# Order of the weight sums on GpSimd and of ScalarE's steps in a hybrid decoder block

## What is computed

```python
h = rmsnorm(x, norm_g)
proj = jnp.einsum('bsd,de->bse', h, w_in)
sb_q, sb_k, sb_v, sb_z, hg_q, hg_f, hg_i, hg_z, gate_logits = jnp.split(proj, split_points, axis=-1)
# stick-breaking attention, per head
z = jnp.einsum('bhqd,bhkd->bhqk', qb, kf) * scale
log_not = jnp.where(causal, jax.nn.log_sigmoid(-z), 0.0)
survive = lax.cumsum(log_not, axis=3, reverse=True) - log_not
w = jnp.exp(jnp.where(causal, jax.nn.log_sigmoid(z) + survive, -jnp.inf))
u_sb = jnp.einsum('bse,ed->bsd', sb_o * jax.nn.silu(sb_z), w_sb_proj)
# HGRN2, per head: a decayed linear attention with state, then rmsnorm
u_hg = jnp.einsum('bse,ed->bsd', hg_o * jax.nn.silu(hg_z), w_hg_proj)
y = gate_sb * u_sb + gate_hg * u_hg
x = x + jnp.einsum('bsd,de->bse', y, w_out)
out = rmsnorm(x, final_norm_g)
```

## Time and profile before

| | us |
|---|---|
| median of 3 runs | 1340.43 |
| lowest and highest | 1339.3, 1341.13 |
| the profiled execution | 1341.63 |
| its span, first to last instruction | 1339.9 |
| TensorE busy | 1320.7 |
| VectorE busy | 918.5 |
| GpSimd busy | 747.0 |
| ScalarE busy | 581.2 |

### The profile page before, as it was taken

One profiled execution on the slowest core, in us unless ns is written; L12 is line 12 of the kernel. 1 busy time (PEld: TensorE's weight loads), 2 busy tenths in 40 slices (PEclk: granted clock), 3 DMA queues, 4 the chain that ended last, 5 costly groups with the idle time before them and its releaser, 6 DMA issues.

```text
span 1339.9 us, 23157 instructions
## 1 busy us (share of the span) xinstructions
PE 1320.7 (99%) x8369; PEld 1101.5 (82%) x8369; DVE 918.5 (69%) x1078; ACT 581.2 (43%) x950; POOL 747.0 (56%) x511
## 2 busy tenths in 40 slices
PE   8999999999999999999999999999999999989998
PEld 7888788888888878888888887888887888878887
DVE  5848877876877887787687788778634446855323
ACT  7553355255345335525534533552444433443222
POOL 5655664554665566455466556645588722787300
PEclk9999999999999999999999999999999999999999
DMA  5121111311112111121111211113544479454602
GB/s 189 32 80 63 33 64 32 94 63 31 63 47 78 63 31 63 31 93 64 31 63 47 78 63 31 63 31 110 183 180 142 156 262 328 142 180 133 228 28 99
DMA packets 132651, 126.98 MB, mean 95 GB/s; under 512 B 4304, under 2 KB 110848, under 8 KB 132608
## 3 DMA queue, kind: packets, MB, share of 16 engines
q1 hardware_dynamic: 124432, 105.13, 24.6%
q10 hardware_dynamic: 8176, 21.26, 4.4%
HBM read 92.82 MB, written 33.55 MB: 94 GB/s over the span
## 4 chain that ended last, share of the span: by engine, by line
PE 79%; POOL 6%; ACT 5%; DVE 4%; issue 3%; DMA 1%; ACTq 0%; SPq 0%; DVEq 0%; POOLq 0%
PE banks L2042 44%; PE banks L2389 6%; PE banks L2337 5%; PE banks L2125 5%; PE banks L2375 5%; PE banks L2103 4%; PE banks L2115 2%; POOL b_lo L787 2%; POOL b_sum L787 2%; ACT b_hi L918 1%; PE banks L2184 1%; PE banks L2089 1%; PE banks L2165 1%; PE banks L2186 1%; PE banks L2179 1%
## 5 line engine op out<-in xcount | busy, mean ns | idle before, releaser
L2042 PE MATMUL banks<-a_hi,b_hi 128*128 128x512 f32 x1064 | 432.0, 406 | 1.7 <-POOL b_lo L787 1.7
L2042 PE MATMUL banks<-a_hi,b_lo 128*128 128x512 f32 x1064 | 416.6, 392 | 0.0
L2042 PE MATMUL banks<-a_lo,b_hi 128*128 128x512 f32 x1064 | 415.3, 390 | 0.0
L787 POOL TENSOR_TENSOR b_lo<-w_raw,b_hi 128x512 fp32r<-128x512 f32 x106 | 159.2, 1513 | 229.9 <-ACT b_hi L918 229.9
L787 POOL TENSOR_TENSOR b_lo<-b_sum,b_hi 128x512 fp32r<-128x512 f32 x114 | 165.7, 1453 | 145.5 <-ACT b_hi L918 145.4
L2042 PEld LDWEIGHTS banks<-a_hi,b_lo 128*128 128x128 f32 x1064 | 199.7, 188 | 44.0
L2042 PEld LDWEIGHTS banks<-a_hi,b_hi 128*128 128x128 f32 x1064 | 200.0, 188 | 41.3 <-POOL b_lo L787 2.9
L2042 PEld LDWEIGHTS banks<-a_lo,b_hi 128*128 128x128 f32 x1064 | 200.4, 188 | 35.8
L918 ACT ACTIVATE b_hi<-b_sum 128x512 fp32r<-128x512 f32 x114 | 71.9, 630 | 145.9 <-POOL b_sum L787 145.6
L787 POOL TENSOR_TENSOR b_sum<-w_raw 128x512 f32<-128x512 f32 x68 | 100.6, 1480 | 0.0
L1101 ACT ACTIVATE wT<-banks 128x512 f32<-128x512 f32 (+2 forms) x96 | 47.1, 491 | 104.5 <-PE banks L2115 88.7
(11 more groups left out here) (256 smaller groups left out, 2620.8 us busy)
## 6 DMA issues: line engine op xcount, KB each, us to landing
w_raw<-in_w_in SPq DMA_DIRECT2D x72, 512.0 KB, 4.9
gate_d<-gate_out SPq DMA_DIRECT2D x16, 512.0 KB, 3.5
x_tok<-in_x SPq DMA_DIRECT2D x8, 512.0 KB, 6.5
z_d<-z_out SPq DMA_DIRECT2D x8, 512.0 KB, 2.7
hz_d<-z_out SPq DMA_DIRECT2D x8, 512.0 KB, 2.7
osb_d<-o_sb SPq DMA_DIRECT2D x8, 512.0 KB, 5.6
ohg_d<-hq SPq DMA_DIRECT2D x8, 512.0 KB, 2.7
w_other<-in_w_in SPq DMA_DIRECT2D x8, 512.0 KB, 5.7
```

The lines of the kernel that those rows point to most:

```text
L787: return nc.gpsimd.tensor_tensor(dst, a, b, op)
L2042: last = mm(bank, w[:, s, k, :], t[s][:, k, :], start=opens and k == 0 and z == 0, stop=k == QUAD - 1 and z == 2, skip_group_check=not opens)
```

## The change

GpSimd now makes T5, T6 and T7 in this order right after the low part of P1, and then the low parts of P6, P7 and P5 in the order of the products. `SPLIT_ORDER` and the numbers of the sums follow this, also in the hg pairs. ScalarE splits P7 at point 10 instead of 7, P5 at 11, P2 at 12 and P3 at 13, one point later each; P6 stays at 9 and P1 at 6. In the hg branch `branch_high` of P2 and P3 stand ahead of the splits of the first hg pair, its split of P7 comes a panel later, and at point 1 the copy of P1's product (and in the first pair `branch_high(P4)`) stands ahead of the split of P4.

```diff
-SPLIT_ORDER = (P1, P7, P6, P5, P2, P3, P4)
+SPLIT_ORDER = (P1, P6, P7, P5, P2, P3, P4)
-RAW_T7, RAW_T5, RAW_T6, RAW_T4 = range(1, 5)
+RAW_T5, RAW_T6, RAW_T7, RAW_T4 = range(1, 5)
@@ prepare (GpSimd), and in the same way hg_prepare
                 split(n, SPLIT_ORDER, P1, raw_block(0, 0, raw))
-                freed(n, P7)
-                sum_t7(n, raw)
-                split(n, SPLIT_ORDER, P7, part_of(b_sum, P7))
                 freed(n, P5)
                 sum_t5(n, raw)
                 sum_t6(n, raw)
+                freed(n, P7)
+                sum_t7(n, raw)
                 freed(n, P6)
                 split(n, SPLIT_ORDER, P6, t2_flat)
+                split(n, SPLIT_ORDER, P7, part_of(b_sum, P7))
                 split(n, SPLIT_ORDER, P5, part_of(b_sum, P5))
@@ pair_point (ScalarE), and in the same way the hg pairs
-                following = {6: P1, 7: P7, 9: P6, 10: P5, 11: P2, 12: P3}
+                following = {6: P1, 9: P6, 10: P7, 11: P5, 12: P2, 13: P3}
@@ branch (ScalarE)
                     hg_split(N_PAIRS, P1)
                     branch_high(P7)
                     branch_high(P5)
+                if t == KT - 1:
+                    branch_high(P2)
+                    branch_high(P3)
+                    hg_split(N_PAIRS, P6)
                     hg_split(N_PAIRS, P7)
-                if t == KT - 1:
-                    hg_split(N_PAIRS, P6)
                     hg_split(N_PAIRS, P5)
                     hg_split(N_PAIRS, P2)
-                    branch_high(P2)
-                    branch_high(P3)
@@ hg pairs (ScalarE)
                     if p == 1:
-                        hg_split(n, P4)
                         act.wait_ge(product_done, PRODUCTS * n + P1 + 1)
                         act.wait_ge(block_taken, 5 * n - 2)
                         copy(hg_u3[:, :], pair_bank(n, P1)).then_inc(p1_copied, 1)
-                    if i == 0 and p == 2:
-                        branch_high(P4)
+                        if i == 0:
+                            branch_high(P4)
+                        hg_split(n, P4)
```

More of the change, by code:

```diff
@@ L795, in sum_t7, with sum_t5 @@
             def sum_t7(n, raw=w_raw):
-                tt(part_of(b_sum, P7), raw_block(0, 1, raw), raw_block(1, 1, raw), ALU.subtract).then_inc(
+                tt(part_of(b_sum, P7), raw_block(0, 1, raw), raw_block(1, 1, raw), ALU.subtract).then_inc(raw_sum, 1)
+            def sum_t5(n, raw=w_raw):
+                tt(part_of(b_sum, P5), raw_block(0, 1, raw), raw_block(0, 0, raw), ALU.subtract).then_inc(
                     raw_sum, FIRST_SUM if isinstance(n, int) and n == 2 else 1)
-            def sum_t5(n, raw=w_raw):
-                tt(part_of(b_sum, P5), raw_block(0, 1, raw), raw_block(0, 0, raw), ALU.subtract).then_inc(raw_sum, 1)
             def sum_t6(n, raw=w_raw):
@@ L890, in hg_prepare @@
                 hg_loaded(pool, n, 1)
-                hg_freed(pool, n, P7)
-                tt(flat(hg_b_sum[P7]), raw_block(0, 1, raw), raw_block(1, 1, raw), ALU.subtract).then_inc(raw_sum, 1)
-                hg_low(n, P7, flat(hg_b_sum[P7]))
                 hg_freed(pool, n, P5)
@@ L897, in hg_prepare @@
                 tt(t2_flat, raw_block(1, 1, raw), flat(hg_b_sum[P5]), ALU.subtract).then_inc(raw_sum, 1)
+                hg_freed(pool, n, P7)
+                tt(flat(hg_b_sum[P7]), raw_block(0, 1, raw), raw_block(1, 1, raw), ALU.subtract).then_inc(raw_sum, 1)
                 hg_freed(pool, n, P6)
                 hg_low(n, P6, t2_flat)
+                hg_low(n, P7, flat(hg_b_sum[P7]))
                 hg_low(n, P5, flat(hg_b_sum[P5]))
```

## The result

The changed kernel takes 1343.87 us (median of 11 runs, 1342.88 to 1345.92) against 1341.13 for the kernel before (11 runs, 1339.30 to 1342.94): a ratio of 1.0023, 95% interval 1.0015 to 1.0031. The forecast was 1339.1, no change. The change makes the kernel slower, by 0.23%, and the time lies inside the range of 1331 to 1344.5 but on the other side of before. The profiled execution took 1342.88 us, its span is 1341.2.

What follows compares the result with a forecast made beforehand. TensorE, busy 1320.7 of 1339.9 us, was taken as the bound. Span: 1339.9 - 2.3 - 6.15 - 0.3 + 7.4 + 0 = 1338.55; the median 1340.43, moved by the same -1.35, gave 1339.1 us, range 1331 to 1344.5.

Steps and rivals of the forecast that it cites:

- gate pairs: Pairs where P6 waited for its low part: the new order makes it 2 to 3 us early, 2.3 us go.
- hg's first pair: First pair of hg's branch: its waits at L2375 and the slow clock after them go, 6.15 us gained.
- start: Kernel start, wait at L2115: 0.3 us gained, with bounds of 0.5 us lost and 2.0 gained.
- v_diff, L2089: Heads, VZ into QF pair: T4 starts 0.10 us before VectorE's v_diff and delays it; 1.06 us lost in seven heads, 7.4 us.
- L2173 and the rest of the heads: Heads, QK into VZ pair: later T4 offset by k_raw coming 0.35 to 1.35 us earlier; 0, bounds -2.3 and +5.2.
- everything behind: The stretch after hg's first pair: no term in the prediction, so 0.
- The rest at nothing: Next pair's raw weights load after T4, up to 4 us later in the QK pair, but are wanted a pair later: 0.
- rival 1: Heads: VectorE gets its operands first at v_diff, so nothing is lost there; 1331.7 us, chance 0.25.
- rival 2: Heads and first gate pairs: T4 behind k_split costs 0.7 to 1.3 us each at L2173; slower, 1345.5 us, chance 0.15.
- the four cases: The forecast (1336.5 to 1342, chance 0.5), rival 1, rival 2, and gains not coming in full in hg's first pair (1342.2, 0.1).

Runs made afterwards that it cites:

- e1: The changed kernel with SyncE's store of gate panel (g-1, 0) issued ahead of the load of weights: 1338.33 us, 0.998 of before.
- e9: The changed kernel with P3's high part back at point 12 in gate pair 33 alone: 1337.81 us, 0.9975 of before.
- e4: The kernel before with only ScalarE's edits in hg's branch: 1340.57 us, 0.9992 of before.
- e8: The changed kernel with ScalarE's edits in hg's branch undone, GpSimd's new order kept: 1347.59 us, 1.0049 of before.
- e3: The changed kernel with P3's high part in the VZ pair made in four pieces, so T4 starts a little later: 1337.71 us, 0.9976 of before.
- e10: The changed kernel with P3's high part back at point 12 in gate pairs 34 to 39, not in 32 and 33: 1344.10 us, 1.0023 of before.
- e2: The changed kernel with P3's high part back at point 12 in the VZ pair alone: 1342.24 us, 1.0005 of before.

## Why the prediction was wrong, step by step

| term | forecast | measured |
|---|---|---|
| gate pairs | -2.3 | +2.76 |
| hg's first pair | -6.15 | -6.14 |
| start | -0.3 | -1.18 |
| v_diff, L2089 | +7.4 | +7.1 (7 x 1.02) |
| L2173 and the rest of the heads | 0 | -1.3 |
| everything behind | 0 | +0.04 |
| sum | -1.35 | +1.30 |

- **Gate pairs: the step that failed.** The gain was there: no wait of the old kind, P6 for its low part, stays in pairs 37 and 38, and in e1 and e9 each of the four pairs takes 19.04 us; their stretch from pair 36 to 40 is 164.47 us, which is -2.5 against before. The failed sentence is "P3's high part moves behind a gate sigmoid that waits for VectorE's c12; P3 is wanted a whole pair later", and with it "The rest at nothing", where T4 was followed to the load of the weights and no further. P3's product does not wait for its operand. But GpSimd makes T4 right behind P3's low part, SyncE's load waits for T4, the store of a gate panel stands behind the load, the sigmoid of the next pair waits for the store to land, and TensorE's P6 waits for that sigmoid: 3.21 us between two matmuls in pair 36 instead of 0.23. P7's low part, which the prediction had 3.7 us early (in pair 37), came 0.8 us too late in pair 36, although TensorE was 3 us late itself. In pair 33 the square roots of `attend_hg(12)` and two table loads stand between points 12 and 13 too; I had counted just these square roots in the heads, and did not ask whether the first gate pairs have them. e9 gave the price of that one place: all of it. e1 gave the price of the queue's order: all of it too. This term alone is off by 5.1 us; without it the sum would have been 2.4 us too high.
- **hg's first pair** was right in size, to 0.01 us, but the reason told only half. I gave it to the copy's place and took GpSimd's order as a condition of pair 40 alone. e4 and e8 show that each part alone gives less than half and that pair 41 would have taken the rest.
- **v_diff** was right in mechanism and size: the lead 0.12 us for 0.10, v_diff 2.26 us for 2.2, seven waits of 1.0 us. The sentence of the Trainium skill that was quoted there (page "SBUF — State Buffer", section "Who interferes with whom") agrees with this trace, and e3 shows it from the other side. That the lead came out at 0.12 us, after a chain of four steps, was close: in e3 a quarter of a microsecond on ScalarE was enough to bring rival 1 about.
- **L2173** was mis-sized, within its bounds. k_raw came at 261.86 instead of 263.51, which is 1.28 us earlier on the head's clock and near the early end of "0.35 to 1.35"; TensorE's start at L2173 comes 0.41 us after the one before it instead of 0.55: 0.14 us in seven heads is 1.0 of the 1.3. Rival 2 did not happen. Its bounds had a slip: eight passages of -0.33 us are -2.6, not -2.3.
- **Start**: 0.3 was forecast with bounds to 2.0. Pair 4 begins at 122.55, 123.25 and 123.30 in the three traces with the old order and between 121.11 and 122.22 in the nine with the new one, 1.2 us earlier in the mean. The wait at L2115 is 0.5 us instead of 1.6: the term was too small by 0.9 us.
- **The slower rival** (rival 2) had the right side and the wrong place. None of the four cases had a transfer as the last to arrive. That the sum of the spans ended only 2.65 us off is in part luck: the gate pairs were 5.1 us worse, the rest 2.4 us better than forecast.

What stays open: what sets the length of the wait of the gate pairs from one execution to the next. The spans of the eleven executions (1341.9 us in the middle, 1341.2 in the profiled one) suggest that it is mostly longer than in the trace shown. How the DMA queues shared is one candidate. TensorE's clock is another: behind the first wait it was down in e8 and e10, where pair 36 took 23.91 and 23.92 us instead of 23.12.

## What to carry over

When a step moves later on one engine, follow it past its own consumer to everything that is counted off it: here a sum, a load that waits for the sum, a store queued behind the load, and a tile that waits for the store. Look for closed loops through a DMA queue whose round is close to the period of the work: here the loop cost nothing until one late T4, and then two pairs paid 5.3 us. In SyncE's lists put the transfer that is ready, and that somebody waits for, ahead of the one that waits.

## What the runs showed of the hardware

**Order at the SBUF, to a tenth of a microsecond.** Of two operations with two SBUF operands on GpSimd and VectorE, the later one lost about 1.0 us whether it came 0.12 us (v_diff, 2.26 us) or 0.15 us (T4, 2.26 us) behind; the first kept its 1.28 to 1.30 us. In e2, where T4 was 0.84 us ahead, v_diff took 1.53 us. In all three cases the later one ended 1.1 us after the first had ended, which is most of what it takes alone (1.23 and 1.27 us). Delaying one operation by 0.25 us in each of seven heads made the kernel 6.2 us faster.

**The length of a wait alone doesn't settle TensorE's clock.** Four stretches of 4 us that begin at the first matmul after a wait (of after, of e8 twice, of e4):

```profile
1006.02:1010.02 4.00, 3.32 (x13) 2.44 (x14) 0.00 (x0) 4.00 (x6) 1.65 (x2) 1.00 0.00 0
```

```profile
1007.05:1011.05 4.00, 4.00 (x11) 3.19 (x12) 0.00 (x0) 4.00 (x6) 1.66 (x2) 0.61 0.00 0
1183.54:1187.54 4.00, 3.00 (x12) 2.14 (x12) 2.89 (x2) 1.49 (x2) 2.38 (x2) 1.00 1.14 322
```

```profile
1188.09:1192.09 4.00, 4.00 (x11) 3.13 (x12) 3.90 (x7) 2.15 (x5) 4.00 (x4) 0.57 0.09 30
```

The starts of matmuls stood 3.2, 3.5, 1.6 and 3.0 us apart at these places. After 3.5 and 3.0 us the granted clock fell towards the lower level (1.2 of 2.4 GHz; matmuls of 512 columns 0.43 us apart instead of 0.23), after 3.2 and 1.6 us it did not. It fell after 3.70 us in e10 too, and stayed at 1.00 after 3.06 us in e2 and 3.47 us in e3. Where it falls, the wait costs more than its length: pair 41 of e4 took 23.56 - 19.04 = 4.52 us extra for a gap of 3.0 - 0.23 us, so 1.75 us of it is the clock. Why it fell after 3.0 us at one place and not after 3.47 at another was not found.
